# Norms by ScalarE's reciprocal square root in a two-layer kernel, and closed chunks copied out one set of exponentials later

## What is computed

```
def _rms(x):
    xf = x.astype(jnp.float32)
    return xf * lax.rsqrt(jnp.mean(xf * xf, axis=-1, keepdims=True) + EPS)
```

## Time and profile before

| | us |
|---|---|
| runs | 2765.63, 2770.78, 2772.05; median 2770.78 |
| profiled execution, its own time | 2769.22 |
| its span | 2767.6 |
| busy PE, DVE, ACT, POOL | 2675.0, 1546.5, 1030.7, 95.9 |
| mean granted TensorE clock | 0.978 of full |

### The profile page before, as it was taken

How to read it: one execution, slowest core, us unless ns; L and a number is a source line. 1 busy time by engine, 2 the same in 40 slices (tenths; PEclk the granted TensorE clock), 3 DMA queues, 4 the chain that set the end, 5 groups by cost and what they waited for, 6 DMA issues and landing times.

```text
span 2767.6 us, 38125 instructions
## 1 busy us (share of the span) xinstructions
PE 2675.0 (97%) x12980; PEld 2153.7 (78%) x12980; DVE 1546.5 (56%) x3652; ACT 1030.7 (37%) x1585; POOL 95.9 (3%) x84
## 2 busy tenths in 40 slices
PE   6999999999999878999999999999999999999999
PEld 4887888887765556888887888888878888888887
DVE  4444444336644855339999999722245555555544
ACT  4344343224313663433334565522233232222321
POOL 0000000002011001000000000000000000000000
PEclk9999999999986999999999999999999999999999
DMA  4222232233310001324443555574564555555452
GB/s 144 87 95 93 85 97 78 92 104 122 122 35 0 1 1 46 107 86 132 138 137 115 205 210 208 197 252 145 147 188 163 210 180 192 198 174 212 156 185 76
DMA packets 97901, 360.57 MB, mean 130 GB/s; under 512 B 9664, under 2 KB 9664, under 8 KB 96528
## 3 DMA queue, kind: packets, MB, share of 16 engines
q1 hardware_dynamic: 75744, 242.25, 27.3%
q0 software_dynamic: 19184, 79.45, 8.1%
q10 hardware_dynamic: 2880, 37.75, 3.5%
HBM read 289.68 MB, written 69.21 MB: 130 GB/s over the span
## 4 chain that ended last, share of the span: by engine, by line
PE 83%; DVE 13%; ACT 3%; issue 1%; DMA 0%; DVEq 0%; POOL 0%; ACTq 0%; POOLq 0%
PE bank L401 23%; PE bank L402 23%; PE bank L403 23%; PE bank L976 4%; DVE wlo L389 2%; PE bank L416 2%; ACT pair_prob L1186 1%; PE bank L492 1%; PE bank L627 1%; PE bank L855 1%; PE bank L646 1%; PE bank L664 1%; DVE eq L1956 1%; DVE sel L1958 1%; DVE eq L1951 1%
## 5 line engine op out<-in xcount | busy, mean ns | idle before, releaser
L401 PE MATMUL bank<-act_hi,whi 128*128 128x512 f32 x1968 | 781.0, 397 | 28.5 <-DVE act_lo L1403 21.6
L402 PE MATMUL bank<-act_lo,whi 128*128 128x512 f32 x1968 | 770.9, 392 | 0.0
L403 PE MATMUL bank<-act_hi,wlo 128*128 128x512 f32 x1968 | 770.0, 391 | 0.0
L389 DVE TENSOR_TENSOR wlo<-raw,whi 128x1024 fp32r<-128x1024 f32 x398 | 485.3, 1225 | 430.4 <-ACT whi L385 428.4
L385 ACT ACTIVATE whi<-raw 128x1024 fp32r<-128x1024 f32 x398 | 417.2, 1053 | 233.1 <-PE bank L403 200.0
L401 PEld LDWEIGHTS bank<-act_hi,whi 128*128 128x128 f32 x1968 | 371.5, 189 | 120.0 <-issue 33.6
L403 PEld LDWEIGHTS bank<-act_hi,wlo 128*128 128x128 f32 x1968 | 371.5, 189 | 78.4
L402 PEld LDWEIGHTS bank<-act_lo,whi 128*128 128x128 f32 x1968 | 371.8, 189 | 73.8 <-issue 0.5
L401 PE MATMUL bank<-h_hi,whi 128*128 128x512 f32 x1024 | 404.4, 395 | 2.9 <-DVE h_lo L1995 2.9
L402 PE MATMUL bank<-h_lo,whi 128*128 128x512 f32 x1024 | 404.3, 395 | 0.0
L403 PE MATMUL bank<-h_hi,wlo 128*128 128x512 f32 x1024 | 404.3, 395 | 0.0
(11 more groups left out here) (321 smaller groups left out, 2292.8 us busy)
## 6 DMA issues: line engine op xcount, KB each, us to landing
raw<-tiles SPq DMA_DIRECT2D x398, 512.0 KB, 3.9
acts_dram<-gelu SPq DMA_DIRECT2D x128, 256.0 KB, 4.1
gates_dram<-stage ACTq DMA_DIRECT2D x8, 4096.0 KB, 12.9
wg<-gates_dram POOLq DMA_DIRECT2D x16, 2048.0 KB, 17.2
hf<-acts_dram POOLq DMA_DIRECT2D x16, 2048.0 KB, 10.9
bias<-alibi POOLq DMA_DIRECT2D x16, 256.0 KB, 3.0
w1s<-cmp_w POOLq DMA_DIRECT2D x1, 4096.0 KB, 13.4
res<-x_t ACTq DMA_DIRECT2D x4, 512.0 KB, 10.1
```

Of the source, the lines that this page charges most:

```text
L389: dve.tensor_tensor(wlo[:, j.slot, :], raw[:, j.slot, :], whi[:, j.slot, :].bitcast(F32), ALU.subtract).then_inc(lo_made, 1)
L401: pe.matmul(bank[j.slot][:, :], wh, hi[:, kc, :], start=(kc == 0), stop=False)
L402: pe.matmul(bank[j.slot][:, :], wh, lo[:, kc, :], start=False, stop=False)
L403: last = pe.matmul(bank[j.slot][:, :], wl, hi[:, kc, :], start=False, stop=(kc == KC - 1))
```

## The change

Sqrt becomes Abs_reciprocal_sqrt at `root` and at L1100; DVE's reciprocal goes, the Newton step stays. The powers at L579, L583 and L585 (two of them) go from GpSimd; in their place ACT takes the reciprocal root and DVE adds three small instructions of a Newton step on at most 64 columns; the last two powers become one step on all 64. The router's power stays. `pair_out` for pair i-2 now stands in iteration i behind the first head's exponentials, and the one for pair 10 behind the loop; `root(4)` keeps its place in the order, with `pair_out(8)` no longer ahead of it.

```diff
+        def of_tiles(n):
+            return lambda t: t[:, 0:64].rearrange("p (t n) -> p t n", t=TT)[:, :, 0:n]
+        SMALL = [of_tiles(14), lambda t: t[0:N_CMP, 0:2], of_tiles(16)]
+        SMALL_MS = [3, 4, 6]
...
@@ gpsimd
-            power(3, 14, view=lambda t: t[:, 0:64].rearrange("p (t n) -> p t n", t=TT)[:, :, 0:14])
             pool.wait_ge(S("hidden_made"), 2)
             pool.dma_start(wuq[:, :, :], w_uq).then_inc(S("wuq_landed"), 16)
             pool.dma_start(wukv[:, :, :, :], w_ukv).then_inc(S("wukv_landed"), 16)
-            power(4, 2, rows=N_CMP)
-            for n in range(2):
-                power(5 + n, 8, view=lambda t: t[:, 0:64].rearrange("p (t n) -> p t n", t=TT)[:, :, 8 * n:8 * n + 8])
...
@@ scalar
-                act.activation(rrow[:, slot, :], bank[b][:, :], ACT.Sqrt, scale=1.0 / width, bias=k("eps"))\
+                act.activation(rrow[:, slot, :], bank[b][:, :], ACT.Abs_reciprocal_sqrt, scale=1.0 / width, bias=k("eps"))\
...
-            act.activation(rrow[:, 1, :], mean[:, :], ACT.Sqrt, scale=-2.0).then_inc(roots_made, 1)
+            act.activation(rrow[:, 1, :], mean[:, :], ACT.Abs_reciprocal_sqrt, scale=-2.0).then_inc(roots_made, 1)
...
+            def small_root(n):
+                act.wait_ge(ms_made, SMALL_MS[n])
+                act.activation(SMALL[n](rstd), SMALL[n](ms), ACT.Abs_reciprocal_sqrt).then_inc(S("small_roots"), 1)
...
             for m in (12, 13):
                 make_hi(act, Job(J_D + m).ahead(RING))
+            small_root(0)
...
+            small_root(1)
             for p in range(20):
...
+            small_root(2)
             act.wait_ge(S("roped"), 15)
             copy(mk[64:96, :, :], krg[64:96, :].unsqueeze(1).broadcast_to((32, 8, T)), S("kr_spread"))
...
+                    if e == 0 and i >= 2:
+                        pair_out(i - 2)
                     pair_copy(i, e)
                 if PAIRS[i]["cmp"] is not None:
                     cmp_copy(PAIRS[i]["cmp"])
-                if i:
-                    pair_out(i - 1)
                 if i == 9:
                     root(4, 0, 7, 512)
+            pair_out(len(PAIRS) - 2)
...
@@ vector
             def invert(n, slot):
-                reciprocal_of(n, slot)
-                improve(n, slot)
-            def reciprocal_of(n, slot):
+                y = rrow[:, slot, :]
                 dve.wait_ge(roots_made, n)
-                dve.reciprocal(rrow[:, slot, :], rrow[:, slot, :]).then_inc(S("newton"), 1)
...
-            dve.wait_ge(rstd_made, 1)
+            def small_newton(n):
+                y, m, t = SMALL[n](rstd), SMALL[n](ms), SMALL[n](prod)
+                dve.wait_ge(S("small_roots"), n + 1)
+                dve.tensor_tensor(t, y, y, ALU.mult).then_inc(S("small_step"), 1)
+                dve.wait_ge(S("small_step"), 2 * n + 1)
+                dve.scalar_tensor_tensor(out=t, in0=t, scalar=-0.5, in1=m, op0=ALU.mult, op1=ALU.mult)\
+                    .then_inc(S("small_step"), 1)
+                dve.wait_ge(S("small_step"), 2 * n + 2)
+                dve.scalar_tensor_tensor(out=y, in0=t, scalar=1.5, in1=y, op0=ALU.add, op1=ALU.mult)\
+                    .then_inc(rstd_made, 1)
+                dve.wait_ge(rstd_made, n + 1)
+            small_newton(0)
...
-            dve.wait_ge(rstd_made, 2)
+            small_newton(1)
...
-            dve.wait_ge(rstd_made, 4)
+            small_newton(2)
...
                 if i == 10:
-                    reciprocal_of(4, 0)
-                    improve(4, 0)
+                    invert(4, 0)
```

More of the change, by code:

```diff
@@ L548, in _, with power @@
                     pool.dma_start(bias[:, e, :], alibi[bass.ds(c * 2 + e, 1), :, :]).then_inc(bias_landed[e], 16)
-            def power(n_ms, n, rows=P, view=None):
+            def power(n_ms, n):
                 pool.wait_ge(ms_made, n_ms)
-                view = view or (lambda t: t[0:rows, 0:n])
-                pool.tensor_tensor(view(rstd), view(ms), view(neg_half), ALU.pow).then_inc(rstd_made, 1)
+                pool.tensor_tensor(rstd[:, 0:n], ms[:, 0:n], neg_half[:, 0:n], ALU.pow).then_inc(rstd_made, 1)
             def add_up(squares, before, chunk):
@@ L1286, in _ @@
             u_job(1)
-            act.wait_ge(rstd_made, 5)
+            act.wait_ge(rstd_made, 4)
             scale_routes(0)
@@ L1369, in invert @@
             def invert(n, slot):
-                reciprocal_of(n, slot)
-                improve(n, slot)
-            def reciprocal_of(n, slot):
+                y = rrow[:, slot, :]
                 dve.wait_ge(roots_made, n)
-                dve.reciprocal(rrow[:, slot, :], rrow[:, slot, :]).then_inc(S("newton"), 1)
-            def improve(n, slot):
-                y = rrow[:, slot, :]
-                dve.wait_ge(S("newton"), 3 * n - 2)
                 dve.tensor_tensor(mend[:, :], y, y, ALU.mult).then_inc(S("newton"), 1)
-                dve.wait_ge(S("newton"), 3 * n - 1)
+                dve.wait_ge(S("newton"), 2 * n - 1)
                 dve.wait_ge(S("means_made"), n)
                 dve.tensor_tensor(mend[:, :], mend[:, :], mean[:, :], ALU.mult).then_inc(S("newton"), 1)
-                dve.wait_ge(S("newton"), 3 * n)
+                dve.wait_ge(S("newton"), 2 * n)
                 dve.scalar_tensor_tensor(out=y, in0=mend[:, :], scalar=1.5, in1=y, op0=ALU.add, op1=ALU.mult)\
```

## The result

The changed kernel took 2748.6 us (median of four runs, 2748.0 to 2752.9) against 2771.1 for the kernel before (four runs): a ratio of 0.9926, with a 95% interval of 0.991 to 0.9941. The forecast was 2755.0 with a range of 2748 to 2762. Two later sessions measured the same kernel again, in five runs each: 0.9934 (0.992 to 0.9948) and 0.994 (0.9927 to 0.9954). Over all 14 runs its median is 2750.6, and that of the kernel before over the three later sessions (37 runs) is 2769.1. So the change is worth 18.5 us, where the sum of the prediction had 15.6. The first four runs alone would have said 22.5.

A forecast was written before the change was run, and what follows sets the result against it. PE bounds the kernel, busy 2675.0 of 2767.6 us, so only its waits pay. Terms of 16.4 us off and 0.8 on, 15.6 net, from 2769.2 give 2753.6; the runs' median lies 1.6 higher, so 2755, range 2748 to 2762.

The forecast's parts named there:

- norm 1: PE waits 9.94 us for the first chunk's rest, ending a chain through the reciprocal; without the reciprocal, 3.39 us gained.
- norms 2 and 3: Both reciprocals precede DVE's first division; PE waits 3.61, 0.25 and 0.46 us for divisions; 4.32 us gained, no more.
- norm 5: Reciprocal stands before PE's second halves of the jobs; a matmul at 1063.74 could start at 1061.37; 2.37 us gained.
- norm 6: PE waits 8.61 us with nothing to do; without the reciprocal, 3.39 us gained.
- norm 4: Reciprocal hidden; a table load slips under ACT's idle time, ahead of copies PE awaits for 7.13 us; 1.30 us gained.
- pairs: Exponentials fill ACT's wait for the mixing; 0.45 to 0.49 us each at pairs 1, 3, 5, 0.15 at 7; together 1.60.
- small norms: Replacing GpSimd's powers: first zero, second 0.06 us slower, the step before PE's awaited diagonals 0.7 slower; 0.8 together.
- Exposed switches: Rival: both added table loads stand on the chain, 2 x 1.28 = 2.6 us, so 2758 us; chance 0.12.
- The slow root: Rival: the new root takes 3.35 us instead of 0.69 on ACT, losing 12.5 us, so 2768 us; chance 0.03.
- the waits did not move: Rival denied here: at norms 2, 3 and 5 ACT's rounding or loads end last, so 2765 us; chance 0.07.
- The clock rises: Rival: less idle at norm 4 lifts PE's clock, 2.1 us for the mixing, as much for transposes; 2751 us; chance 0.12.
- The signs: Trace signs if right: first job about 28.8, norm 4 wait about 5.7, after norm 6 5.2, pair period 20.9 us.

## Why the prediction was right, and where its terms were off

The forecast of 2755.0 was high by 6.4 against the first four runs and by 4.4 against all 14, within its range each time; its chance of 0.86 for faster by over 0.3% was on the right case. The sum of the direct terms, 15.6, was right almost by accident, since two terms were off in opposite directions; and the 2.8 us that the runs gained beyond it had no term at all:

```
term                 forecast   measured
norm 1                 3.39       3.40
norms 2 and 3          4.32       5.11
norm 5                 2.37       2.47
norm 6                 3.39       3.39
norm 4                 1.30       1.50
pairs                  1.60       0.56
small norms           -0.8       -0.77 (up to the diagonals)
sum                   15.6       15.7
```

The 0.56 of the pairs is that of the kernels with GpSimd's power. The small norms can be seen once more in the rows of the diagonals and the pairs together: the changed kernel stands 0.7 to 0.9 behind the one with the powers there.

**Norms 1 and 6** were waits that DVE's chain ended before and after, and a wait like that is worth exactly the instruction that goes.

**Norms 2 and 3**: "PE has other jobs until 699.1, so it cannot gain more than these waits" was wrong by 0.79. The idle times of the earlier trace rows add up to 4.32, but PE lost more than its idle time at each. Where PE ran on without a wait, its matmuls came 0.227 us apart. Across the first wait the starts were 4.00 apart, the 0.39 of the matmul ahead and the 3.61 of idle time, so the wait cost 3.77; and the matmul behind it was 0.47 long instead of 0.39 and held the next one up by another 0.08. In the traces the three steps are 3.84, 0.49 and 0.74 against idle times of 3.61, 0.25 and 0.46, about 0.25 more each. Where a wait only becomes shorter, as at norms 1 and 6, this extra stays. Norm 5, which was worked out from starts instead of idle times, came within 0.1. The lead of DVE was as forecast in kind: `divide(0)` moved from 701.88 to 691.22.

**Pairs**: the step that failed is that "the pattern repeats every 21.4 us" for pairs 1, 3 and 5, each worth 0.45 to 0.49. Pairs 1 and 3 gave 0.28 each, 5 and 7 nothing. There are two errors in it. The copies do not start 0.43 us behind PE's transposes but 0.58, in the changed kernel at pair 3:

```profile
945.01 0.60 ACT L1113 ACTIVATE sqo<-bank 128x512 f32<-128x512 f32 x1 [0.57 <-PE bank L505]
...
947.29 0.88 PE L416 MATMUL bank<-con,pair_prob 128*128 128x128 f32 x6
947.87 0.87 ACT L1110 ACTIVATE pair_prob<-bank 128x384 f32<-128x384 f32 x2 [1.78 <-PE bank L416]
```

ACT is idle for 1.78 us there, so the engine is free, as forecast, and PE is what ends last. And behind the mixing of pair 5 come the scores of pair 9, a latent pair, not of a grouped one. The kernel before, at that place:

```profile
981.11 2.87 PE L453 MATMUL bank<-mk,mq 96*128 96x128 f32 x12
981.23 0.60 ACT L1108 ACTIVATE sqo<-bank 128x512 f32<-128x512 f32 x1 [2.74 <-PE bank L499]
...
983.82 0.82 PE L416 MATMUL bank<-con,pair_prob 128*128 128x128 f32 x6
984.38 0.85 ACT L1105 ACTIVATE pair_prob<-bank 128x384 f32<-128x384 f32 x2
```

The copy began 0.56 us behind the transposes before anything was changed, against 0.88 in the earlier trace rows. ACT's wait of 2.74 us cost nothing at this pair. One look at the second half of the supposed pattern would have shown it.

**Norm 4**: the mechanism held whole. The load ran ahead of its wait (998.34, with the root at 1003.69), `pair_out(8)` moved behind the exponentials, and the wait came to 5.64 where "about 5.7" stood (7.13 less the 1.30 of the sum would be 5.83). Most of the further 0.2 is `pair_out(8)`: 0.95 us from its start to the copies behind it, against 1.10 from its start to the load before. The run with the order of the pairs alone shows that nothing but the order did it.

**Small norms**: the first cost nothing, the second nothing where 0.06 was forecast (the diagonal of the compressed keys moved by 10.65 us, and DVE's instructions ahead of it by 10.64), the third 0.77 where 0.7 was. ACT loaded the table long before `ms` was made and ran the first small root at once (first lines below); the others are the third root's Newton step and the diagonals behind it:

```profile
754.66 1.28 ACT L1107 ACT_TABLE_LOAD   x1
...
765.36 0.25 ACT L1107 ACTIVATE rstd<-ms 128x56 f32<-128x56 f32 x1 [9.42 <-DVE ms L1630]
765.64 0.22 DVE L1636 TENSOR_TENSOR prod<-rstd 128x56 f32<-128x56 f32 x1 [0.32 <-ACT rstd L1107]
...
871.23 0.21 DVE L1636 TENSOR_TENSOR prod<-rstd 128x64 f32<-128x64 f32 x1
871.48 0.22 DVE L1638 SCALAR_TENSOR_TENSOR prod<-prod,ms 128x64 f32<-128x64 f32 x1
871.74 0.22 DVE L1641 SCALAR_TENSOR_TENSOR rstd<-prod,rstd 128x64 f32<-128x64 f32 x1
872.00 0.18 DVE L1801 TENSOR_SCALAR rq_b<-rstd 128x32 f32<-128x32 f32 x1
872.09 1.65 DVE L1653 TENSOR_SCALAR diag<-con,rstd 128x128 f32<-128x128 f32 x8
```

The three steps start 0.26 us apart, and DVE is busy without a break into the diagonals. Against GpSimd's power this part of the change is a loss, if a small one: it removes 21.2 us of POOL's busy time that nobody waited for.

**The rivals.** Exposed switches: no added load stood on the chain. At norm 4 a load of 1.283 us lay under ACT's idle time and cost nothing; and the loads for the first two small roots ran 10 us ahead of them, as the lines above show for one. The Trainium skill, page "ScalarE: Activation LUTs", section "What ACT_TABLE_LOAD costs", gives about 2.66 us for every switch, 1.28 of it the load and 1.38 a drain. The load agrees (1.283 here). Of a drain these rows show nothing: in the kernel before, the load at norm 4 stood at 1018.81, and the root began 0.02 us behind its end. The estimate of 2760 had both switches exposed; as neither was, the time does not test it. The slow root is out (684 ns), the waits did not move, and in the changed kernel no mixing between pairs 1 and 8 took more than 2.40 us. It can happen, though: in the first profile of the kernel with the row norms alone one of them took 4.07 us, and the pairs' row lost 1.86. *The clock rises* was the rival closest to what was left over, but in the wrong place. At norm 4 it did rise, and the mixing fell from 4.54 to 3.36 us. It was worth 1.0 to 1.2 us there, where the rival had put twice 2.1. In all three profiles a further 3.2 us went in two stretches that the change does not touch, the w1 matmuls (1.64) and the row sums (1.6). Set against one profile of the kernel before, this makes the clock the likely cause of the 2.8 us beyond the sum, but does not show it term by term. The forecast had no term for stretches outside the edit. That 2750.6 still lies in its range is owed to the 4 us that this rival had added to it at another place.

**The signs.** The waits at norms 4 and 6 (5.64 and 5.22), the loads and the root came as said. The first job started at 28.35 instead of 28.8, since the kernel's first 19 us were 0.57 shorter in this profile. The grouped pairs repeat every 21.13 us, not every 20.9: that sign failed with the term of the pairs.

## What to carry to other kernels

A wait counts from start to start of the matmuls around it, not by its idle time alone: three short waits were worth 5.11 us where their idle times gave 4.32. Before a gain is multiplied by the number of repetitions, look at the last repetitions too: two of four had another shape and gave nothing. And ACT's idle time just before a wait is the place for a table load (three of them lay there in the changed kernel and cost nothing): put the instruction that needs the table first behind the wait, and order work that does not need the awaited result ahead of it.

Where a kernel has stages of narrow matmuls, a difference of two or three us in the whole shows little about an edit. Compare the starts of the same matmuls in both traces, stretch by stretch, and profile one of the programs twice.

## What the runs showed of the hardware beyond what was expected

PE's granted clock moved between its two levels in the same program from run to run (products stage at 0.52 or 0.63, 3.3 us apart), and the changed times of such stretches came in steps of about 1.6 us: 15.85, 17.5 or 19.1 us for the same 64 one-column matmuls and what surrounds them. Such steps can hide an edit in the whole time: a version whose trace had 4.7 us less of a wait was 1.8 us faster by the means of 10 and 14 runs. What decides between the steps was not found.

The last loop took 704.1 or 707.0 us, 0.4% apart, with PE never idle and the granted clock at 1.00 in both. It was the one or the other throughout an execution (704.1 in eight of the fourteen profiles, 707.0 in six), and five programs showed both. What decides it was not found.
